# Other byte places for the seven weight forms of the feature stage, three of them interleaved word by word

## The reference

```
shift, scale, gate = split(silu(c) @ w_ada + b_ada)
h    = x * (1 + scale) + shift                  # x: (2048 + 64) x 1024
proj = h @ w_in                                 # queries, keys, values, gates, conv inputs
A    = windowed attention of three groups (dilations 1, 4, 16), times silu(gate), @ w_out_a
B    = gated delta rule behind a width-4 convolution, times silu(gate), @ w_out_b
out  = (sigmoid(ga) * A + sigmoid(gb) * B) @ w_o
y    = LayerNorm(alpha * x + gate * out)
```

## Time and profile before

| | |
|---|---|
| median of 3 runs | 2392.25 us (2389.87, 2392.25, 2394.27) |
| profiled execution: span from the first to the last instruction | 2390.6 us |
| PE, PEld busy | 2286.9 us (96%), 2049.0 us (86%) |
| DVE, ACT, POOL busy | 1633.5 us (68%), 1166.9 us (49%), 373.8 us (16%) |
| matmuls of L320 | 7308 of 16842 |

### The profile page before, as it was taken

One profiled execution on the slowest core, in us unless ns is written; L12 is line 12 of the kernel. 1 busy time (PEld: TensorE's weight loads), 2 busy tenths in 40 slices (PEclk: granted clock), 3 DMA queues, 4 the chain that ended last, 5 costly groups with the idle time before them and its releaser, 6 DMA issues. The chain is left out here.

```text
span 2390.6 us, 45041 instructions
## 1 busy us (share of the span) xinstructions
PE 2286.9 (96%) x16842; PEld 2049.0 (86%) x16842; DVE 1633.5 (68%) x4008; ACT 1166.9 (49%) x2457; POOL 373.8 (16%) x627
## 2 busy tenths in 40 slices
PE   5999999999999999999999989889998899999998
PEld 2778788888899999999999978668887799999786
DVE  5877776555363676776645569669987877778797
ACT  4444445444421554444444468647776533333554
POOL 0010000000111011110000001123321035445100
PEclk8999999999999999999999999969999699999999
DMA  7232323332532233223333367966565556667563
GB/s 270 97 115 97 115 98 115 106 106 88 190 119 75 93 106 119 93 96 112 111 110 105 107 253 244 360 179 172 148 187 176 191 180 209 189 189 234 190 213 124
DMA packets 256969, 363.56 MB, mean 152 GB/s; under 512 B 55654, under 2 KB 191438, under 8 KB 252272
## 3 DMA queue, kind: packets, MB, share of 16 engines
q1 hardware_dynamic: 197408, 224.24, 30.3%
q0 software_dynamic: 36496, 124.94, 13.6%
q10 hardware_dynamic: 22848, 11.50, 1.8%
HBM read 246.94 MB, written 113.68 MB: 151 GB/s over the span
## 5 line engine op out<-in xcount | busy, mean ns | idle before, releaser
L320 PE MATMUL ps_f<-m_lo,w_hi 128*128 128x272 f32 (+1 forms) x2436 | 789.5, 324 | 11.6 <-DVE m_lo L648 6.1
L320 PE MATMUL ps_f<-m_hi,w_hi 128*128 128x272 f32 (+1 forms) x2436 | 794.2, 326 | 0.0
L320 PE MATMUL ps_f<-m_hi,w_lo 128*128 128x272 f32 (+1 forms) x2436 | 785.3, 322 | 0.0
L320 PEld LDWEIGHTS ps_f<-m_lo,w_hi 128*128 128x128 f32 x2436 | 459.5, 189 | 51.8 <-issue 16.5
L320 PEld LDWEIGHTS ps_f<-m_hi,w_lo 128*128 128x128 f32 x2436 | 460.3, 189 | 37.3
L320 PEld LDWEIGHTS ps_f<-m_hi,w_hi 128*128 128x128 f32 x2436 | 459.2, 189 | 33.9
L712 DVE TENSOR_TENSOR stage<-partial,ps_f 128x512 f32<-128x512 f32 (+2 forms) x348 | 183.1, 543 | 308.5 <-PE ps_f L320 298.8
L453 ACT ACTIVATE partial<-ps_f 128x272 f32<-128x272 f32 (+1 forms) x348 | 161.0, 463 | 375.1 <-PE ps_f L320 373.7
L415 ACT ACTIVATE w_hi<-w_raw 128x512 fp32r<-128x512 f32 x348 | 212.5, 625 | 194.6 <-PE ps_f L320 113.7
L619 DVE TENSOR_TENSOR w_lo<-w_raw,w_hi 128x512 fp32r<-128x512 f32 x348 | 238.8, 687 | 84.7 <-ACT w_hi L415 80.7
L738 DVE SCALAR_TENSOR_TENSOR conv<-stage,side,conv 128x1024 f32<-128x1024 f32 x108 | 138.2, 1279 | 8.3 <-ACT conv L469 7.1
(11 more groups left out here) (772 smaller groups left out, 4716.1 us busy)
## 6 DMA issues: line engine op xcount, KB each, us to landing
w_raw<-in_w_feat SPq DMA_DIRECT2D x58, 1024.0 KB, 5.9
gates<-scratch_g_d SPq DMA_DIRECT2D x56, 256.0 KB, 3.4
m_rows<-scratch_parts_d SPq DMA_DIRECT2D x16, 768.0 KB, 4.7
z_f<-scratch_z_d ACTq DMA_DIRECT2D x13, 768.0 KB, 6.6
scratch_conv_d<-conv POOLq DMA_DIRECT2D x18, 544.0 KB, 3.0
scratch_conv_d<-conv POOLq DMA_DIRECT2D x18, 512.0 KB, 2.9
kc<-in_k_cache SPq DMA_DIRECT2D x8, 1152.0 KB, 11.6
vc<-in_v_cache POOLq DMA_DIRECT2D x8, 1152.0 KB, 9.3
```

The lines of the kernel that those rows point to most:

```text
L320: last = pe.matmul(out[:, 0:n], l[:, cols], r, start=start and k == 0 and nth == 0, stop=k == KH - 1 and nth == 2, skip_group_check=not start)
```

## The change

The fourteen tiles become one tile, `w_forms`, of 7432 words (before, 7168 in all). Each form's parts are slices of it: `W_AT` holds, per form, the word at which the high part begins, the word of the low part, and the step between two words of a part. Against the old places, the first three moved forms stand 64, 288 and 528 bytes further on, with their words next to each other as before. The last three ("22", "s4", "s3") stand 768, 832 and 1056 bytes further on, and their step is 2: high word, low word, high word, and so on. Form "11" stays. Counted from a multiple of 128 bytes the seven now begin at 32, 96, 64, 48, 32, 96 and 64 bytes.

`w_sum` still lies on the low part of form "s2". What follows the forms in memory begins 1056 bytes later. Every engine issues the same instructions with the same sizes, waits and signals in the same order as before; only addresses and, for three forms, the step of ACT's output, of DVE's input and output and of PE's stationary operand differ.

```diff
+W_AT = ((0, 512, 1), (1040, 1552, 1), (2120, 2632, 1), (3204, 3716, 1), (4288, 4289, 2), (5328, 5329, 2), (6408, 6409, 2))
+W_WORDS = W_AT[-1][0] + 2 * KH * P
...
-            sb("w_place", [P, 4 * KT * P + 7 * KH * P], where=early)
+            sb("w_place", [P, 4 * KT * P + W_AT[3][1]], where=early)
             w_sum = sb("w_sum", [P, KH * P], where=early)
         with ExitStack() as early:
             raw = sb("w_raw", [P, 2, 2, KT * P], where=early)
-            wh, wl = [], []
-            for j in range(7):
-                wh.append(sb(f"w_hi{j}", [P, KH * P], F32R, early))
-                wl.append(sb(f"w_lo{j}", [P, KH * P], F32R, early))
+            w_forms = sb("w_forms", [P, W_WORDS], F32R, early)
+            wh, wl = ([w_forms[:, w[n]:w[n] + w[2] * (KH * P - 1) + 1:w[2]] for w in W_AT] for n in range(2))
...
-        sb("w_rest", [P, 4 * KT * P + 14 * KH * P - 5 * KT * VW])
+        sb("w_rest", [P, 4 * KT * P + W_WORDS - 5 * KT * VW])
```

## The result

The changed kernel takes 2395.9 us (median of 20 runs, 2390.68 to 2403.26), the kernel before 2392.32 (20 runs beside them). The ratio is 1.0023 [1.0014, 1.0032]: slower by 5.5 us [3.3, 7.7]. (The two medians differ by 3.6 us and the means by 4.9, both inside this interval.) The forecast was 2392 and no change; the time lies inside the range, but no change is excluded. One run of either kernel says nothing on so small a difference, so what follows leans on the rhythm of matmuls inside one trace, and on ratios of several runs where there are any. Rhythm means the time from one start to the next; in pass 0 it repeats to a nanosecond from trace to trace, in pass 1 to some 15 ns in the 21,100 of a pair.

A forecast was written before the change was run, and what follows sets the result against it. The prediction took the feature stage L320 to be bound by PE's matmul start rate; places, step and splits each counted 0 on the 2390.6 us span, and the runs' median, 1.65 us above, gave 2392 us, range 2374 to 2438.

The forecast's parts named there:

- The places: Feature stage L320, both passes: new byte places of six forms' weights change the extra per matmul by 0, spread +-5 us.
- the disturbed feed: Rival, forms "22", "s4", "s3", both passes: step 2 makes the time beyond the columns come twice, 43 us, 2435 us; chance 0.24.
- places that win: Rival, L320: all six moved forms fall to the trace's lowest extra, 10.0 ns; 24 us faster, 2368 us; chance 0.24.
- places lose a little: Rival, L320: the contiguous forms or all six get a higher extra, 5 to 29 us, about 2405 us; chance 0.07.
- The bounds: L320, six moved forms: limits on the places' effect, taken from extras in other rows and a mirrored gap, -24 to +29 us.
- The step of 2: PE's weight reads in three interleaved forms: taken as 0, since loads have room under the matmuls.
- The halved load: Rival, interleaved forms in pass 1: weight load takes twice as long per column and becomes the bound, 180 us, 2572 us; chance 0.07.
- The splits: ACT and DVE writing interleaved forms: at most 0.41 us more each, hidden behind PE's matmuls, taken as 0.
- the cover: Splits run ahead of PE's matmuls; thinnest where pass 1 begins, still covered; without it 1 us, once.
- The test that was set: L320 rhythm: prediction wrong if any form moves more than about 1 ns in both passes without another moving the other way.

## Why the prediction was wrong

- **The places, the step that failed.** "I take 0, with +-5 as its own spread" was the term. With the change's places and no step, pass 0 lost 160 ns a pair, 4.6 us, and pass 1 won 1.3. The prediction argued that signs mix and went by the weights' own place past a multiple of 128. What counts is the distance to the moving operand, which rows 4 to 6 could not show, since both operands differ there. The equal extra of all seven forms, read as a sign that only the lowest bits of the address count, was equal distance. That the old distance is the best of those tried in pass 0 made the signs not mix: moves to 16, 32 and 64 all cost there. The time lies inside the stated range because the range was wide for other reasons, the disturbed feed and places that win; that is no support for the mechanism. The rival that held, "places lose a little", had 5 to 29 us and a chance of 0.07; it had the size, but not the mechanism.
- **The bounds** (-24 to +29 us for six forms) held: the weights alone moved by 32, the worst distance for pass 0, cost 9.8 us. For the places that win by 24 us no distance was found: the best gain of any was 3.4 us, in pass 1, with a larger loss in pass 0.
- **The step of 2**, taken as 0, is about 3 us by the rhythm at the old places (the ratio, 1.0010 [0.9999, 1.0022], allows that and nothing) and, beside the change's places, 0 in pass 0 and 3.1 us in pass 1. "The step disturbs the feed" was right in kind and named the point from which it decides, but its price of 16.4 and 12.6 ns was seven times too high in pass 0 and more in pass 1. The page "Advanced Engine Details and Errata" of the Trainium skill, section "Memory Cachelines", would put the step of 2 at nothing, since each line is still hit twice. The 2.4 ns a matmul and the 195 ns of a load against 189 are small, but not nothing.
- **The halved load** fell: loads of the changed kernel last 192 ns, with all six forms interleaved 195.
- **The splits**, taken as 0, cost the time of ACT (649 ns in the mean of all, some 48 more for an interleaved one, against the 410 more of rows 11) and none of DVE, and the cover held: PE idles before L320 for nothing that a split releases.
- **The test that was set** ("wrong if any form's rhythm moves by more than about 1 ns in both passes without another that moves the other way") was just met, by "22" and "s3": they rose by 1.8 and 4.2 ns a matmul in pass 0 and by 1.0 each over the two units of pass 1, and nothing fell by as much. "s1" rose by 4.2 ns in pass 0, but by 0.1 in pass 1; the pair's 62 ns there are 0.4 ns a matmul.
- **What stays open.** Why two reads at one distance disturb each other, and why the best distance differs between 512 and 272 columns. The rhythm of the kernel with the places alone gives 3.3 us where its time gives 8.1 [5.0, 11.0]. Part of that is the clock of the runs: its eight had a mean granted clock of 0.9739, the 19 beside them 0.9755, and between runs of one kernel the time falls by some 1.3 us for each 0.001 (an estimate from the 142 runs here that were taken in groups of seven or more). That is some 2 us of the difference; the rest was not located. That the two operands' reads meet in memory fits all the runs here, but no run shows the meeting itself.

## What to carry to other kernels

Where matmuls load new weights each time at the full clock, the place of a tile is a parameter of the kernel: compare the starts of the same matmul in two traces before the times, and look at the distance between stationary and moving operand, not at either address; here its value within 128 bytes counted most. Where a loop reads one operand at several offsets, as pass 1 does, each has its own distance. A change that opens, widens or reorders tiles ahead of such a stage moves this distance by accident; here that was worth up to 0.4% of the kernel, and 0.2% in the change itself. Test a place in a kernel in which all matmuls of the loop have it, since neighbours carry over.

## What the runs showed of the hardware

- The time between starts of 512-column matmuls with a weight load each goes from 230.0 to 234.4 ns (2760 to 2813 for 12) with the distance of their two operands, at the granted clock 1.00; 128 bytes further on it is the same again (one kernel). At 0.50 the distance that is worst at 1.00 still runs at 426.7, the columns alone. With 272 columns, 128 bytes are not a full period (84 matmuls: 10,550 ns at 64, 10,593 at -64).
- Moving both operands together leaves every form and both units as they were, to the nanosecond. The Trainium skill, page "SBUF — State Buffer", section "Who interferes with whom", gives PE one read port for the moving operand and one for weight loads, independent of each other, and says that PE waits for no one; by that the distance would cost nothing. The 9.8 us [6.5, 13.4] of the kernel with the weights alone moved say that the two reads are not independent in time here.
- A form's rhythm depends on its neighbours: an unmoved form ran at 2753 to 2769 ns beside moved ones, against 2760, and the gaps at its two ends changed most.
- ACT writes 512 words with a step of 2 in some 672 ns instead of 625; DVE, which reads and writes with it, takes 689 instead of 687. A weight load with that step takes 195 ns instead of 189 (six forms interleaved).
